# Expert stage of a two-layer decoder trunk: experts ranked by token count on the chip, five of 128 slots with split products, three of 64 slots in plain fp32 on two column tiles, weights addressed by register

## What is computed

```python
def moe_ffn(x, w_router, wg, wu, wd):
    logits = (xt @ w_router).astype(jnp.float32)
    top_v, top_i = lax.top_k(logits, TOP_K)          # TOP_K = 2 of N_EXPERTS = 8
    w = jax.nn.softmax(top_v, axis=-1)
    gates = jnp.sum(jax.nn.one_hot(top_i, N_EXPERTS, dtype=jnp.float32) * w[..., None], axis=1)
    for e in range(N_EXPERTS):
        y = y + gates[:, e:e + 1].astype(xt.dtype) * swiglu(xt, wg[e], wu[e], wd[e])
```

## Time and profile before

| | |
|---|---|
| runs | 1580.91, 1584.02, 1584.55 us (median 1584.02) |
| span of the profiled execution | 1579.9 us; its own time isn't listed apart from the three |
| busy share of the span | PE 96%, PEld 77%, DVE 71%, ACT 61%, POOL 2% |
| expert stage | 578 to 1562 us, eight experts of 122.85 us |
| read from HBM | 439.30 MB, of them 352 MB expert weights (336 issues of 1024 KB) |

### The profile page before, as it was taken

The page is one execution under the profiler, slowest core; times in us unless marked ns, Lnnn a source line. Parts: engine busy times, 40 slices in busy tenths (PEclk is TensorE's granted clock), DMA queues, the critical chain, the costliest instruction groups (busy, mean ns, idle before and its releaser), DMA issues.

```text
span 1579.9 us, 17806 instructions
## 1 busy us (share of the span) xinstructions
PE 1518.0 (96%) x7063; PEld 1222.6 (77%) x7063; DVE 1122.6 (71%) x960; ACT 956.7 (61%) x920; POOL 35.4 (2%) x73
## 2 busy tenths in 40 slices
PE   8989999999998979999999999999999999999996
PEld 6775788887777467888888888888888888888874
DVE  4523544544452359888888888888988888888895
ACT  5443543343434246677777777677767777777773
POOL 2000000000000000000000000000000000000010
PEclk9979999999997989999999999999999999999998
DMA  9520855555242069999999999999999999999991
GB/s 346 180 107 1 293 186 187 187 187 185 85 160 107 1 239 338 350 348 382 360 348 382 365 343 385 369 329 377 378 345 365 393 329 374 387 338 360 398 403 75
DMA packets 148628, 445.24 MB, mean 282 GB/s; under 512 B 9406, under 2 KB 21564, under 8 KB 148540
## 3 DMA queue, kind: packets, MB, share of 16 engines
q1 hardware_dynamic: 146836, 438.24, 75.6%
q0 software_dynamic: 1584, 5.77, 0.9%
q10 hardware_dynamic: 120, 0.04, 0.0%
HBM read 439.30 MB, written 4.72 MB: 281 GB/s over the span
## 4 chain that ended last, share of the span: by engine, by line
PE 89%; DVE 5%; ACT 4%; issue 1%; DMA 0%; DVEq 0%; SPq 0%; POOLq 0%; POOL 0%; ACTq 0%
PE bank L689 86%; PE bank L692 3%; DVE part_l L1560 3%; ACT part_h L1204 1%; DMA ring<-in_w_in_dram 0%; ACT junk L1213 0%; DVE gm L1565 0%; DVE gg L1565 0%; DVE xT L1564 0%; ACT prob L1398 0%; ACT probT L1204 0%; ACT in_h L1204 0%; ACT pxh L1204 0%; DVE y L1560 0%; DVE in_l L1560 0%
## 5 line engine op out<-in xcount | busy, mean ns | idle before, releaser
L1560 DVE TENSOR_TENSOR part_l<-ring,part_h 128x2048 fp32r<-128x2048 f32 x378 | 859.3, 2290 | 189.3 <-ACT part_h L1204 186.7
L1204 ACT ACTIVATE part_h<-ring 128x2048 fp32r<-128x2048 f32 x378 | 721.3, 1919 | 235.7 <-PE bank L689 235.1
L689 PE MATMUL bank<-part_h,xh 128*128 128x512 f32 x1120 | 447.6, 400 | 6.9 <-DVE part_l L1560 3.2
L689 PE MATMUL bank<-part_h,xl 128*128 128x512 f32 x1120 | 437.7, 391 | 0.0
L689 PE MATMUL bank<-part_l,xh 128*128 128x512 f32 x1120 | 436.5, 390 | 0.0
L689 PEld LDWEIGHTS bank<-part_h,xh 128*128 128x128 f32 x1120 | 210.3, 188 | 59.9 <-DVE part_l L1560 15.1
L689 PEld LDWEIGHTS bank<-part_h,xl 128*128 128x128 f32 x1120 | 210.2, 188 | 46.2
L689 PEld LDWEIGHTS bank<-part_l,xh 128*128 128x128 f32 x1120 | 210.7, 188 | 41.1
L689 PE MATMUL bank<-part_h,hTh 128*128 128x512 f32 x560 | 221.2, 395 | 3.6 <-DVE hTl L1560 2.6
L689 PE MATMUL bank<-part_h,hTl 128*128 128x512 f32 x560 | 218.9, 391 | 0.0
L689 PE MATMUL bank<-part_l,hTh 128*128 128x512 f32 x560 | 218.8, 391 | 0.0
(11 more groups left out here) (262 smaller groups left out, 978.7 us busy)
## 6 DMA issues: line engine op xcount, KB each, us to landing
ring<-in_moe_w_gate_dram SPq DMA_DIRECT2D x112, 1024.0 KB, 7.2
ring<-in_moe_w_up_dram SPq DMA_DIRECT2D x112, 1024.0 KB, 7.3
ring<-in_moe_w_down_dram SPq DMA_DIRECT2D x112, 1024.0 KB, 7.1
ring<-in_w_in_dram SPq DMA_DIRECT2D x7, 2048.0 KB, 7.9
ring<-in_dense_w_gate_dram SPq DMA_DIRECT2D x14, 1024.0 KB, 5.1
ring<-in_dense_w_up_dram SPq DMA_DIRECT2D x14, 1024.0 KB, 5.1
ring<-in_dense_w_down_dram SPq DMA_DIRECT2D x14, 1024.0 KB, 4.9
ring<-in_w_o_dram SPq DMA_DIRECT2D x4, 2048.0 KB, 7.7
```

What stands on the lines that cost most here:

```text
L689: return nc.tensor.matmul(o, lhsT, rhs, start=start, stop=stop)
L1204: return nc.scalar.activation(dst, src, ACT.Copy, scale=scale)
L1560: return nc.vector.tensor_tensor(o, a, b, op)
```

## The change

At compile time the eight places in the order are named wide or narrow: `NARROW` makes places 1, 3 and 5 narrow. Expert 0 always has place 0, since its loads start before the routing is known. The other seven are ranked by their token count on DVE; the four with most tokens take the wide places 2, 4, 6 and 7, the three with fewest the narrow ones. `order_i` holds which expert stands at each place; SP reads it into a register ahead of each place's loads and adds it to the DRAM address of each DMA.

A wide place works as before. A narrow place has `FEW` = 64 slots. Its pieces aren't split: `narrow_piece` multiplies straight from `ring` with plain fp32 operands (`xn`, `hTn`), and its matmuls go in turn to PSUM partitions 0 to 63 and 64 to 127, that is to two column tiles of 64. For gate and up the two tiles take the two halves of a chunk's columns, for down the two halves of the 1024 outputs. SP waits for `s_used` before it overwrites a narrow piece. `silu`, product, turn and copy of a narrow chunk handle 128 x 512 values once instead of twice, and there is no low part of them. An expert with more tokens than its place holds goes to the loop after the eighth place, which takes its slots from `cap`.

```diff
-    SLOTS = P
+    SLOTS, FEW = P, P // 2
+    NARROW = (False, True, False, True, False, True, False, False)
+    NARROWS = sum(NARROW)
+    RANK_AT = [a for a in range(E) if not NARROW[a]] + [a for a in range(E) if NARROW[a]]
     MAX_OVER = 2 * SEQ // (SLOTS + 1)
+    assert len(NARROW) == E and not NARROW[0] and not NARROW[E - 1] and RANK_AT[0] == 0
+    MOE_NARROW = [NARROW[m // MC] for _, m, _ in MOE_ORDER]
+    WIDE_J = [j for j in range(len(MOE_ORDER)) if not MOE_NARROW[j]]
+    WIDE_N = {j: n for n, j in enumerate(WIDE_J)}
+    assert len(WIDE_J) == (E - NARROWS) * PIECES
+    def turns_before(m, low=False):
+        return sum((1 if NARROW[i // MC] else MOE_CHUNKS[i % MC][1] // W) for i in range(m)
+                   if not (low and NARROW[i // MC]))
+    def rounds_before(a, low=False):
+        return sum((1 if NARROW[i] else 2) for i in range(a) if not (low and NARROW[i]))
+    def rows_before(a):
+        return sum((FEW if NARROW[i] else SLOTS) for i in range(a))
...
             def load_experts():

+                expert = [0] * E
                 for j, (part, m, i) in enumerate(MOE_ORDER):
-                    e, (c, n) = m // MC, MOE_CHUNKS[m % MC]
+                    a, (c, n) = m // MC, MOE_CHUNKS[m % MC]
+                    if a and (part, m, i) == (0, MC * a, 0):
+                        if a == 1:
+                            sp.wait_ge(m_ord, 1)
+                        expert[a] = sp.value_load(order_i[0:1, a:a + 1], min_val=0, max_val=E - 1)
                     if j < 2 * RING:
                         sp.wait_ge(*reader(MIX * L - RING + j // 2))
-                    sp.wait_ge(s_hi, PIECES + j - 2 * RING + 1)
-                    sp.wait_ge(s_lo, PIECES + j - 2 * RING + 1)
+                    elif MOE_NARROW[j - 2 * RING]:
+                        sp.wait_ge(s_used, PIECES + j - 2 * RING + 1)
+                    else:
+                        sp.wait_ge(s_hi, PIECES + WIDE_N[j - 2 * RING] + 1)
+                        sp.wait_ge(s_lo, PIECES + WIDE_N[j - 2 * RING] + 1)
+                    w = (moe_w_gate, moe_w_up, moe_w_down)[part]
+                    w = w[0, bass.ds(expert[a], 1), :, :].rearrange("o k n -> (o k) n") if a else w[0, 0]
                     if part < 2:
                         k = KT * W // 2 // n
-                        src = (moe_w_gate, moe_w_up)[part][0, e, i * k * P:(i + 1) * k * P, c:c + n]
+                        src = w[i * k * P:(i + 1) * k * P, c:c + n]
                     else:
                         k = 2
-                        src = moe_w_down[0, e, c + i * k * P:c + (i + 1) * k * P, :]
+                        src = w[c + i * k * P:c + (i + 1) * k * P, :]
                     sp.dma_start(piece_in[j % (2 * RING)].rearrange("p (k n) -> p k n", k=k),
                                  src.rearrange("(k p) n -> p k n", p=P)).then_inc(landed[j % (2 * RING)], 16)
...
+            for r, a in enumerate(RANK_AT):
+                pool.memset(rank_at[:, r:r + 1], float(a))
+                pool.memset(row_at_rank[:, r:r + 1], float(rows_before(a)))
...
             for e in range(E - 1):
                 pool.wait_ge(m_ye, e + 1)
-                pool.dma_start(parked[e * P:(e + 1) * P, :], ye).then_inc(m_park, 16)
-            pool.wait_ge(m_park, 16 * (E - 1))
+                if NARROW[e]:
+                    for side in range(2):
+                        pool.dma_start(parked[rows_before(e):rows_before(e + 1), side * W:(side + 1) * W],
+                                       ye[side * FEW:(side + 1) * FEW, 0:W]).then_inc(m_park, 16)
+                else:
+                    pool.dma_start(parked[rows_before(e):rows_before(e + 1), :], ye).then_inc(m_park, 16)
+            pool.wait_ge(m_park, 16 * parks_before(E - 1))
...
+                if e and r == 0 and NARROW[e - 1]:
+                    pe.wait_ge(m_xe, rounds_before(e))
+                elif e:
+                    pe.wait_ge(m_xl, rounds_before(e, low=True) + r)
+                if NARROW[e]:
+                    for k in range(KT):
+                        for b in range(NB):
+                            last = mm(bank[7][:, k * FEW:(k + 1) * FEW], xs[:, b, k * P:(k + 1) * P],
+                                      gm[:, b, 0:FEW], b == 0, b == NB - 1)
+                    last.then_inc(m_xep, 1)
+                    return
...
+                if half == 0 and m and NARROW[(m - 1) // MC]:
+                    pe.wait_ge(m_hTh, turns_before(m))
+                else:
+                    past(pe, m_hTl, turns_before(m, low=True) + half)
+                for k in range(MOE_CHUNKS[m % MC][1] // (2 * P) if NARROW[m // MC] else 4):
                     last = turn(bank[6][:, k * P:(k + 1) * P], hid[:, half, k * P:(k + 1) * P])
...
+            def narrow_piece(j):
                 part, m, i = MOE_ORDER[j]
                 e, n = m // MC, MOE_CHUNKS[m % MC][1]
-                cs = slice((e % 2) * P, (e % 2 + 1) * P)
-                pe.wait_ge(s_lo, PIECES + j + 1)
-                wh, wl = part_h[:, j % PARTS, :], part_l[:, j % PARTS, :]
+                wide = n // 2
+                w = piece_in[j % (2 * RING)]
                 if part < 2:
                     ks = KT * W // 2 // n
                     if i == 0 and part == 0:
                         if m % MC == 0:
-                            pe.wait_ge(m_xl, 2 * (e + 1))
+                            pe.wait_ge(m_xe, rounds_before(e + 1))
+                        pe.wait_ge(m_sg, m)
+                    if i == 0 and part == 1:
+                        pe.wait_ge(m_hid, m)
+                    pe.wait_ge(landed[j % (2 * RING)], 16 * ((PIECES + j) // (2 * RING) + 1))
+                    for k in range(ks):
+                        for t in range(2):
+                            kk_, at_ = i * ks + k, k * n + t * wide
+                            last = mm(bank[2 * part][t * FEW:(t + 1) * FEW, 0:wide], xn[:, kk_, :],
+                                      w[:, at_:at_ + wide], kk_ == 0, kk_ == KT - 1)
+                else:
+                    if i == 0:
+                        pe.wait_ge(m_hTh, turns_before(m + 1))
+                    if i == 0 and m % MC == 0:
+                        pe.wait_ge(m_ye, e)
+                    pe.wait_ge(landed[j % (2 * RING)], 16 * ((PIECES + j) // (2 * RING) + 1))
+                    for k in range(2):
+                        for side in range(2):
+                            kk_, at_ = 2 * i + k, k * D + side * W
+                            t, c = divmod(kk_, wide // P)
+                            last = mm(bank[4][side * FEW:(side + 1) * FEW, :],
+                                      hTn[:, c * P + t * FEW:c * P + (t + 1) * FEW], w[:, at_:at_ + W],
+                                      m % MC == 0 and kk_ == 0, m % MC == MC - 1 and kk_ == n // P - 1)
+                last.then_inc(s_used, 1)
+            def moe_piece(j):
+                part, m, i = MOE_ORDER[j]
+                e, n = m // MC, MOE_CHUNKS[m % MC][1]
+                if NARROW[e]:
+                    narrow_piece(j)
+                    return
+                cs = slice((e % 2) * P, (e % 2 + 1) * P)
+                pe.wait_ge(s_lo, PIECES + WIDE_N[j] + 1)
+                wh, wl = part_h[:, WIDE_N[j] % PARTS, :], part_l[:, WIDE_N[j] % PARTS, :]
...
             def split_moe(j):

                 act.wait_ge(landed[j % (2 * RING)], 16 * ((PIECES + j) // (2 * RING) + 1))
-                act.wait_ge(s_used, PIECES + j - PARTS + 1)
-                copy(part_h[:, j % PARTS, :], piece_in[j % (2 * RING)]).then_inc(s_hi, 1)
+                act.wait_ge(s_used, PIECES + WIDE_J[WIDE_N[j] - PARTS] + 1)
+                copy(part_h[:, WIDE_N[j] % PARTS, :], piece_in[j % (2 * RING)]).then_inc(s_hi, 1)
...
+                act.wait_ge(m_xep, rounds_before(e) + r + 1)
+                if NARROW[e]:
+                    for k in range(KT):
+                        i = copy(xn[:, k, :], bank[7][:, k * FEW:(k + 1) * FEW], columns("ffn", KT * (L - 1) + k))
+                    i.then_inc(m_xe, 1)
+                    return
...
+                ts(stays[:, :], place[:, :], float(E - 1), None, ALU.is_lt)
+                link(tt(keep[:, :, :], rsg[:, 0], cap[:, None, :].to_broadcast(wide), ALU.is_lt))
+                link(tt(keep[:, :, :], keep[:, :, :], stays[:, None, :].to_broadcast(wide), ALU.mult))
+                link(tt(rank_hot[:, :, :], rank_hot[:, :, :],
+                        row_at_rank[:, None, :].to_broadcast([P, E, E]), ALU.mult))
+                link(nc.vector.tensor_reduce(row_base[:, :], rank_hot[:, :, :], AX_X, ALU.add))
+                link(tt(kval[:, :, :], row_base[:, None, :].to_broadcast(wide), rsg[:, 0], ALU.add))
...
+            square = [P, E, E]
+            link(nc.vector.scalar_tensor_tensor(out=rank_key[:, :], in0=total[:, :], scalar=float(E),
+                                                in1=rank_key[:, :], op0=ALU.mult, op1=ALU.add))
```

(31 more changed lines are left out.)

105 lines of the change are left out of this document (65 added, 40 removed).

## The result

The changed kernel takes 1541.56 us (median of 1536.52, 1539.77, 1543.35 and 1545.01), the kernel before 1582.79 beside it: ratio 0.9745, with an interval of 95% from 0.9725 to 0.9764. The prediction was 1533, its range 1512 to 1564. So it is faster as forecast, by 41 us where 51 were expected; the forecast's error of 8.6 us is a fifth of the gain. The profiled execution took 1543.35, its span is 1541.6. The span came out 13.2 us above its own forecast of 1528.4. The forecast of the median was set 4.6 us above that of the span, while the profiled execution's time lies only 1.75 us above its span; that the median missed by less than the span is luck.

The account below looks back on a forecast made before the run. PE was taken to bound the kernel, DMA close behind. Gains of 56.6 (narrow stretches) and 6.0 (down pieces), less 10.5 (exits) and 0.6 (small terms), made 51.5: span 1528.4, median 1533 us, range 1512 to 1564.

Parts of the forecast that it names:

- The bound: Narrow experts: bound by DMA, 2.58 us per piece against PE's 1.74, so most of PE's saving is not seen.
- A narrow piece on PE, 1.74: Narrow piece's matmuls: 3.47 us in a row, two column tiles overlapping about completely, so 1.74 us.
- A narrow piece on DMA, 2.58: Transfer of a narrow 1024 KB piece: 2.58 us at 407 GB/s, 2.53 and 2.70 at the ends.
- The entry: Wide to narrow: six pieces issued ahead, queue empty until about 1.9 us, seventh piece lands at 6.9 us.
- 6.9 + 36 x 2.58 = 99.8 us: Narrow stretch: when the next wide piece lands, one step after the last narrow one.
- The exit: Narrow to wide: split 4.2 us, PE goes on at 104.0; standing some 5 us lowers the clock, costing 2.5 each.
- Stalls of the first wide pieces: Start of each wide stretch behind a narrow one: split without lead, pieces pushed back, 1 us each, 3 together.
- Small terms: Ranking, token-row table, memsets and register loads: mostly hidden, 0.6 us taken off the gain.
- No more than now: Expert-stage DMA: 364 to 366 GB/s is a ceiling, 2.88 us per piece, some 1578 us; chance 5%.
- The clock falls in the narrow stretches: PE in narrow stretches: bursts bring the lower clock, a piece averages 3.04 us, end about 1616; chance 3%.
- The tiles don't overlap: Every narrow piece on PE: 3.47 us, 28.9 us lost per narrow expert, 1671 in all; chance 5%.
- ninth pass: After the eighth place: a narrow expert with over 64 tokens brings an extra pass, near 1660 us; chance 2%.

Follow-up runs that it names:

- e2: Changed kernel with each DMA of a narrow place fetching only half of its 1024 KB piece, PE's work the same; 1480.73 us.
- e1: Changed kernel with all eight places wide, keeping ranking, register addresses and token-row table; 1585.58 us, 1.0027 of the kernel before.
- e6: Changed kernel with narrow places 1, 2, 3 instead of 1, 3, 5 and two buffers of xn; 1544.27 us, 0.9771 of the kernel before.
- e7: Changed kernel with five narrow places (1, 2, 3, 5, 6), two buffers of xn and filled exits; 1511.92 us, 0.9582 of the kernel before.

## Why the prediction came out as it did

**The bound.** Right. Narrow experts are bound by DMA; shown by e2 (less to transfer, and 20 us per stretch go) and by the chain (66% transfers).

**A narrow piece on PE, 1.74.** Right: 8 x 0.219 = 1.75.

**A narrow piece on DMA, 2.58.** Right in an undisturbed stretch (2.586). In the stretch behind an entry it is (803.6 - 713.6) / 34 = 2.65, 34 x 0.07 = 2.3 us more. The row of these 90 us says that the engines were not slower:

```profile
713.60:803.60 90.00, 74.49 (x362) 29.90 (x358) 10.96 (x22) 10.56 (x19) 0.80 (x1) 0.98 1.03 408
```

The landings of the single pieces say where the time is. Nearly all of the 34 follow each other by 2.56 us, a little less than forecast. One comes 4.84 us after the one before it, 2.28 more than usual, and that is the one beside the previous expert's parked output (issued at 726.7, landed at 735.1). By its bytes, 0.5 MB, that output is 1.3 us; in the two other stretches 1.2 us are lost at this place, and what the further 1 us was in the first one stays open. The four pieces of the last chunk come 2.71 us apart: their rows are 512 columns, 2 KB, and from 777 to 789 us DMA moved 391 GB/s where it moved 409 from 744 to 776. Neither the parked output nor the shorter rows were in the sum. This is read from the traces, no experiment tried it.

**The entry.** The place of the loss was right, its size was not: piece 9 should have landed at 6.9 + 2 x 2.58 = 12.1 and landed at 13.6 (14.0 and 14.7 in the two other stretches). The queue never ran empty: the sixth piece landed 4.4 us after the stretch began, not before 1.9. The seventh, issued at 701.94, took 5.9 us and not 5.0, and the next two followed by 2.8 and 2.9 and not by 2.58. With so few pieces in flight DMA isn't full. Microsecond by microsecond (columns as in the stretch tables):

```profile
701.00:702.00 1.00, 1.00 (x8) 0.19 (x4) 0.00 (x0) 0.00 (x0) 0.00 (x0) 1.00 1.02 410
702.00:703.00 1.00, 1.00 (x8) 0.55 (x9) 0.00 (x0) 0.47 (x1) 0.00 (x0) 1.00 0.49 164
703.00:704.00 1.00, 1.00 (x8) 0.33 (x6) 0.69 (x1) 0.12 (x1) 0.00 (x0) 1.00 0.77 160
704.00:705.00 1.00, 1.00 (x6) 0.29 (x4) 0.00 (x0) 0.00 (x0) 0.00 (x0) 1.00 0.91 348
...
709.00:710.00 1.00, 1.00 (x8) 0.34 (x6) 0.00 (x0) 0.00 (x0) 0.00 (x0) 1.00 0.60 193
```

There is a second dip at 709, which the prediction had not. 1.5 us more. With the 2.3 this is the 3.8 us by which the next wide piece landed late (103.6 instead of 99.8), and that is nearly all of the error: **what was mis-sized is "6.9 + 36 x 2.58 = 99.8 us"**, in which DMA runs full from the seventh piece on and carries only weights. It is one term, too small by 4 us in 100, three times.

**The exit.** Split 4.2: 4.3. Gap some 5: 4.87. The clock fell behind it as forecast, at a price of 2.0 us where 2.5 was taken. Stalls of the first wide pieces: taken as 1 each; a wide place with a filled exit is 121.2 to 121.8 where 122.8 less 2 x (2.75 - 1.75) makes 120.8, so 0.4 to 1.0. The wide experts, forecast at 121 to 125, came at 123.1 to 124.4.

**Small terms.** Registers and memsets: nothing seen in the places' lengths, as taken, though e1 as a whole is some 2 us dearer than place 0 explains. The ranking hid behind DVE's wait for ACT, as taken. Place 0 lost 2.4 instead of 0.3: 1.6 by the clock, 0.5 more by the split behind the gather.

**The rivals.** "No more than now" fell with 407 GB/s. The 358 GB/s per core that the Trainium skill gives (DMA: Bandwidth & Descriptors, Specifications), by which the three places could have won nothing, is half of what two cores share, 716, and the same page's section Bandwidth has 425 for a core whose neighbour is idle. The kernel here runs on one core, and its 407 fit that; no run here shows the rate with both cores at work. "The clock falls in the narrow stretches" fell as far as the pauses between transfers go: PE's 0.6 us did not bring it down (e6's second narrow place and e7's 200 us are at 1.00 throughout). It did fall, for 3.4 to 6.8 us, at each entry of the first trace, behind the wait for the split, without a price that shows. The Trainium skill's warning (TensorE: Matmul & The Clock Gate, HAM oscillation) is told of waits longer than these pauses; it applied to the waits at the entries and to the exits' 4.87 us, and 1616 didn't follow from it. "The tiles don't overlap" fell with 0.219 us per record. No ninth pass was seen.

## What to carry to other kernels

Before making one engine's work smaller, work out the time of the next bound for the same piece, and look for a stretch of the same trace in which that resource already runs free: its rate there (407 GB/s here) was right to 1%, where the rate that it shows under another bound (366) says nothing about its limit. The losses that a rate doesn't hold are at the seams: count for each entry and exit what is in flight, what lands when, and what else uses the queue. And a gap on PE can cost more than itself by the clock: here 4.87 us cost 2.0 more where PE was the bound behind it, and waits of 2.6 to 4.3 us cost nothing more where DMA was. Where such a gap can't be closed, work that nobody reads can fill it.

## What the runs showed that was not expected

- Two column tiles of 64 overlap completely at 512 plain fp32 columns (0.219 us per record against 0.433), in both orders of the two tiles' matmuls that were tried, so that a weight piece that costs 2.75 us in three rounded products costs 1.75.
- A gap of 2.12 us before the first wide piece left the clock alone at two exits and not at the third, in one execution.
- Waits of 2.6 to 4.3 us at the entries brought the clock down too, though not each time (3.60 us left it alone once), and cost nothing, since DMA is the bound there.
- Filling a gap with work that nobody reads made the wide place behind it faster by 2.0 us and the kernel by some 0.3%, though PE does more work.
- DMA stayed at 407 GB/s over 200 us, with PE working beside it and parked rows written; pieces with rows of 2 KB instead of 4 came every 2.71 us instead of 2.56.
